# Combining two softmax maps while they are turned: identity and a diagonal of ratios on TensorE, in place of a VectorE pass over the keys

## The reference, cut to what matters

```python
s1 = jnp.einsum('bqhd,bkhd->bhqk', q1, k1).astype(F32) * scale
s2 = jnp.einsum('bqhd,bkhd->bhqk', q2, k2).astype(F32) * scale
...
p = jax.nn.softmax(s1, axis=-1) - lam * jax.nn.softmax(s2, axis=-1)
return jnp.einsum('bhqk,bkhv->bqhv', p.astype(v.dtype), v)
```

## Time and profile before

| | us |
|---|---|
| median of three runs | 4312.25 |
| the runs | 4308.04, 4312.25, 4312.65 |
| span of the profiled execution | 4303.9 |
| busy: PE, DVE, ACT, POOL | 3099.8, 2705.5, 1511.1, 1254.2 |
| mean granted TensorE clock | 0.80 |

### The profile page before, as it was taken

How to read it: one execution, slowest core, us unless ns; L and a number is a source line. 1 busy time by engine, 2 the same in 40 slices (tenths; PEclk the granted TensorE clock), 3 DMA queues, 4 the chain that set the end, 5 groups by cost and what they waited for, 6 DMA issues and landing times. The chain is left out here.

```text
span 4303.9 us, 48708 instructions
## 1 busy us (share of the span) xinstructions
PE 3099.8 (72%) x15864; PEld 1982.7 (46%) x15864; DVE 2705.5 (63%) x7617; ACT 1511.1 (35%) x3085; POOL 1254.2 (29%) x1068
## 2 busy tenths in 40 slices
PE   6787798887788769778887679768776677733333
PEld 4676565665555337455554347444433254400000
DVE  1326357337667884477668873577678945776775
ACT  3533366312255651114555540223446611010010
POOL 0000111112233332333223332333334323355553
PEclk8888888898888779898888889888778788855555
DMA  7485767687989989998999899989999999999998
GB/s 261 157 305 189 278 243 267 254 319 307 357 343 375 360 309 390 404 415 354 363 362 366 351 359 384 417 344 402 375 372 386 363 410 415 398 408 415 416 406 336
DMA packets 269363, 1499.17 MB, mean 348 GB/s; under 512 B 44968, under 2 KB 81672, under 8 KB 97464
## 3 DMA queue, kind: packets, MB, share of 16 engines
q0 software_dynamic: 152064, 1107.36, 64.5%
q1 hardware_dynamic: 117048, 388.70, 24.0%
HBM read 1463.49 MB, written 31.36 MB: 347 GB/s over the span
## 5 line engine op out<-in xcount | busy, mean ns | idle before, releaser
L1698 POOL DMA_INDIRECT rt_ring<-in_peer_uv,rt_few_idx x1056 | 1250.9, 1185 | 3021.0 <-PE rt_acc L876 2385.5
L1644 DVE SCALAR_TENSOR_TENSOR rt_ring<-rt_ring,rt_h 128x1024 f32<-128x1024 f32 x1056 | 1265.9, 1220 | 504.7 <-DMA rt_ring<-in_peer_uv,rt_few_idx 481.7
L876 PE MATMUL rt_acc<-rt_ring,rt_diag 128*32 128x512 f32 x4224 | 759.9, 795 | 623.1 <-DVE rt_diag L1655 622.1
L625 PE MATMUL pair<-dense,w 128*128 128x256 f32 (+2 forms) x3056 | 598.6, 355 | 14.0 <-DMA w<-in_weights 12.2
L625 PEld LDWEIGHTS pair<-dense,w 128*128 128x128 f32 x3056 | 518.1, 199 | 128.8 <-issue 64.5
L614 PE MATMUL pair<-w,dense 128*128 128x256 f32 (+1 forms) x2352 | 556.4, 395 | 9.5 <-DVE dense L1300 3.5
L1199 ACT ACTIVATE rt_act_dot<-rt_dot 128x2 f32<-128x2 f32 x528 | 106.1, 202 | 1269.0 <-DVE rt_ring L1644 1262.1
L876 PEld LDWEIGHTS rt_acc<-rt_ring,rt_diag 128*32 128x32 f32 x4224 | 100.1, 122 | 953.4 <-DVE rt_diag L1655 810.1
L614 PEld LDWEIGHTS pair<-w,dense 128*128 128x128 f32 (+1 forms) x2352 | 436.2, 189 | 158.8 <-issue 72.9
L1655 DVE TENSOR_SCALAR rt_diag<-cst,rt_act_dot,rt_few_prob 128x32 f32<-128x32 f32 x1056 | 266.1, 296 | 119.9 <-ACT rt_act_dot L1199 109.5
L625 PE MATMUL bank<-dense,w 128*128 128x256 f32 (+2 forms) x1424 | 276.9, 351 | 1.7 <-DMA w<-in_weights 1.2
(11 more groups left out here) (241 smaller groups left out, 3248.5 us busy)
## 6 DMA issues: line engine op xcount, KB each, us to landing
w<-in_weights SPq DMA_DIRECT2D x284, 1024.0 KB
rt_ring<-in_peer_uv,rt_few_idx POOLq DMA_INDIRECT x1056
dense<-scratch_mod SPq DMA_DIRECT2D x18, 512.0 KB, 12.4
dense<-in_x_prompt SPq DMA_DIRECT2D x16, 512.0 KB, 13.5
rt_h<-scratch_h SPq DMA_DIRECT2D x33, 128.0 KB
rt_x<-scratch_x SPq DMA_DIRECT2D x132, 32.0 KB
out_k_prompt<-dense SPq DMA_DIRECT2D x32, 128.0 KB
out_v_prompt<-dense SPq DMA_DIRECT2D x32, 128.0 KB
```

The costliest lines, as they stand in the source:

```text
L625: mm = nc.tensor.matmul(bank[b][:, 0:n], wt[:, k * CH + j * P:k * CH + (j + 1) * P], src[:, k, 0:n], start=(k == 0), stop=(k == KC - 1))
L876: mm = nc.tensor.matmul(acc[u % 2][a * T:(a + 1) * T, :], diag[b % 2][:, i, :], slot[:, D + c * BANK:D + (c + 1) * BANK], start=(q == 0), ...
L1644: dt = nc.vector.scalar_tensor_tensor(up, up, 1.0, h2[u % 2][:], ALU.mult, ALU.mult, accum_out=dot[:, b % 2, i:i + 1])
L1698: nc.gpsimd.indirect_dma_start(ring[n % RING][:], None, d["peer_uv"], bass.IndirectOffsetOnAxis(ap=few_idx[u % 2][:, c:c + 1], axis=0)).th ...
```

## The change

The VectorE pass over all keys is replaced by a scaling of the 128x128 identity by the column of ratios. It is kept in the place of the four lambda vectors among the constants (256 columns, two diagonals of 128), which are read only at the start. For each key tile PE now accumulates two matmuls into the same place: the first map times the identity, and the second map times the diagonal of ratios. Both give the turned tile; their sum is the turned combined map. The first map is no longer overwritten.

```diff
+        lamd = consts["lam"].rearrange("p (a c) -> p a c", a=2)
...
                     for kt, w in key_tiles(t)[first:first + 4]:
-                        tr = nc.tensor.transpose(bank[4][0:w, (kt - first) * P:(kt - first) * P + n],
-                                                 prob[0:n, x % 2, 0, kt * P:kt * P + w], ident[0:n, 0:n])
+                        turned = bank[4][0:w, (kt - first) * P:(kt - first) * P + n]
+                        nc.tensor.matmul(turned, prob[0:n, x % 2, 0, kt * P:kt * P + w], ident[0:n, 0:n], start=True, stop=False)
+                        tr = nc.tensor.matmul(turned, prob[0:n, x % 2, 1, kt * P:kt * P + w], lamd[0:n, x % 2, 0:n], start=False, stop=True)
                     tr.then_inc(at_turned, 1)
...
                     settle(nc.vector.scalar_tensor_tensor(ratio[0:n, c:c + 1], recip[0:n, x % 8, 1:2], nlam[0:n, :], total[0:n, c, 0:1],
                                                           ALU.mult, ALU.mult))
-                    nc.vector.scalar_tensor_tensor(prob[0:n, c, 0, 0:nk], prob[0:n, c, 1, 0:nk], ratio[0:n, c:c + 1], prob[0:n, c, 0, 0:nk],
-                                                   ALU.mult, ALU.add).then_inc(at_mixed, 1)
+                    nc.vector.tensor_scalar(lamd[0:n, c, 0:n], ident[0:n, 0:n], ratio[0:n, c:c + 1], None, ALU.mult).then_inc(at_mixed, 1)
```

More of the change, by code:

```diff
@@ L1473, in attend @@
                     t = GROUPS[g][units[x][1]]
-                    n, nk, c = width(t), key_count(t), x % 2
+                    n, c = width(t), x % 2
                     dve.wait_ge(at_exped[0], base + x + 1)
```

## The result

The changed kernel takes 4332.02 us (median of 7 runs, 4320.23 to 4342.82) against 4308.42 us (7 runs, 4292.09 to 4312.74) for the kernel before beside it: a ratio of 1.0054, 95% interval 1.0035 to 1.0072. It is 24 us slower. The forecast was slower, and by 59 us: the sign was right and the size more than twice too large. The profiled execution spans 4330.2 us, 26.3 us more than the 4303.9 of before.

What follows compares the result with a forecast made beforehand. Attention's loop, with PE and DVE handing work to each other and neither full, was taken as the bound. Turning +88, DVE -9, clock -20 gave +59 us, 4371 us; own range 4337 to 4439, start lowered to 4310.

Steps and rivals of the forecast that it cites:

- Where the time is: Attention stretches, 721.6 us together: only they change, and their loss or gain reaches the end nearly whole.
- The price of a turned tile: PE's turning in attention: one record becomes four, 0.50 us more per full tile, 152 us of PE work in all.
- The share on the path: Attention: of 152 us added turning, 88 us lengthen the run; the rest hides in PE's waits.
- first parts: Turn parts before the last, groups 2 to 4: 64 us, mostly hidden beside the diag wait, 16 us counted.
- DVE's part: Attention: pass over keys replaced by identity scaling, 42 us less DVE work, mostly hidden, -9 us on the path.
- The clock: PE in attention: busier PE is granted 0.80 instead of 0.75, other work shrinks 25 us, -20 us on the path.
- rival 3: Attention: full PE clock pays for the turns, 70 - 9 - 49 = +12, 4324 us; chance 0.15.
- Rival 1: Attention: nothing absorbed, every added record on the path at 0.59 us per tile, no clock help, 4485 us; chance 0.08.
- rival 2: Attention: DVE is the bound, turns run in PE's idle time, 42 us go, 4270 us; chance 0.08.
- Rival 4: Turning line: identity matmul still comes out as one record, halving the added work, +20 us; chance 0.02.

Runs made afterwards that it cites:

- e1_pe_only: Kernel before, DVE pass kept, each key tile turned by two float32 identity matmuls (four records) instead of one transpose: ratio 1.0079, 34 us slower.
- e9_six_records: Kernel before, DVE pass kept, each key tile turned by three float32 identity matmuls (six records): ratio 1.0186, 80 us slower.
- e4_dve_only: Kernel before without the DVE pass, diagonal built, only the first map turned by one transpose, second map left out: ratio 0.9982, 8 us faster.

## Why the prediction was wrong in size

**Where the time is: right.** Attention took the whole 26.3 us, and the rest of the program gave none of it back in sum.

**The price of a turned tile: mis-sized.** I took 0.50 us, between 0.40 and 0.73, and measured, by the turning lines of e1_pe_only and the earlier trace rows, (174.4 - 63.8)/288 = 0.38 us:

```profile
L763 PE MATMUL bank<-cst,dense 128*128 128x128 f32 x1152 | 174.4, 308 | 26.1 <-ACT dense L1126 17.0 <-ACT dense L1150 7.4 <-DVE dense L1482 1.5
...
L763 PE MATMUL bank<-cst,dense 32*128 32x32 f32 x128 | 15.9, 274 | 0.9 <-ACT dense L1150 0.9
```

With the 40 small tiles, 13.0 us (15.9 above and 2.5 for the smallest form, less 5.4 before), that is 124 us in place of 152. Two things were wrong. The bounds of 0.40 and 0.73 came from eight records of L805 less four of L760, 0.53 and 0.97 us; that difference also holds the longer start of the one line, and it was tripled. By the timeline of the changed kernel a pair of records takes 0.22 or 0.43 us, a record half of that, so three records more are 0.33 us at the fast pace and 0.64 at the slow one. The prediction's own pitch of 0.11 or 0.21 us gives the same. And the work that was added raised the clock at which it ran, so the fast pace counts for more.

**The share on the path: right in total.** 88 of 152 us was 0.58, and 0.58 is what e9_six_records measured for the step from four records to six. That they agree to the second digit is luck, since the parts were guessed. At the measured size this term is about 69 us in place of 88. Inside it the first parts of groups 2 and 4 hid nearly fully and those of group 3 didn't.

**DVE's part: right in size, partly by luck.** -9 forecast, -8 measured with e4_dve_only, although the diagonal cost 289 ns and not 226. But 5 of the 9 us were to come in group 1, whose stretch shrank by 0.3 us; groups 2 and 4 gave 5.3 and 4.7, and group 3 was 2.4 us longer.

**The clock: mis-sized.** I wrote "I put 0.80 for after, my guess between the two rows" and took -20 us. The stretches were granted 0.81 to 0.87, the rest of PE shrank by 40.5 us and not by 25, and by the estimate above 34 us of it reached the end. I gave rival 3's mechanism the weight of a small correction. Its full form (0.40 for a tile, 49 us back, +12) was too hopeful in turn: the waits for exponentials stayed and the clock didn't reach 1. The result lies between the two, 12 us above the rival and 35 below the forecast.

So two terms of the sum failed, in size and not in kind: the price of the turned tiles, about 19 us too high on the path, and the clock, about 14 us too small. Put together with the runs' terms: 69 - 34 - 8 = +27, against 26.3 in the trace and 24 by the medians. The first two are not apart from each other: 69 - 34 is the 35 us of e1_pe_only, split by the share of 0.58. Rival 1 (no absorption) and rival 2 (DVE bounds, faster) both fell: the first by the 0.58, the second by e4_dve_only, where 38 us less of DVE work brought 8. Rival 4 fell by the four records.

## What to carry to other kernels

On an engine that pauses often, price added work twice: what it adds times the share on the path, and what its clock then gives back to all other work there. Here the second term took half of the first, by the estimate above. It doesn't go on: from four records to six the clock rose no further and the full share was paid, so measure one step beyond the change before trusting a cheap first step. And price a few more records by the pitch of one pace in one line, not by the difference of two lines. And work taken off an engine that waits for another one mostly becomes waiting: ask what releases the instruction behind it.

## What the runs showed that was not expected

Useless matmuls in PE's waits made the kernel before faster: 95.3 us of them brought 7 us (ratio 0.9983, and 0.9984 in a second kernel with still more of them), while the granted clock went from 0.72 to 0.78 up to 0.78 to 0.86. And transposes held the clock up as well as float32 matmuls did, 0.81 to 0.86 with four transposes for each tile.
